# Identity-times-ones matmuls put ahead of five waits of TensorE in a hybrid decoder layer

## The chip, the cores and the metric

The kernel runs on one core of one Trainium2 chip. The metric is the device time of one execution in microseconds (us): 2514.37 us is the median of three runs of the kernel before, which took 2513.86, 2514.37 and 2521.84 us.

## The reference, cut to what matters

One decoder layer is applied to 576 tokens (a prompt of 512 and 8 sampled sequences of 8) with a model width of 2048, all in float32:

```
xn = rmsnorm(x, n1g);  z = xn @ w_in                  # 2048 x 6152
y_conv = rmsnorm(bg * conv3(cg * xt), conv_g)         # short gated convolution
h = mlstm(q, k, v, li, lf);  y_ml = sigmoid(o) * rmsnorm(h, ml_g)
x = x + concat(y_conv, y_ml) @ w_out
hn = rmsnorm(x, n2g)
x = x + (silu(hn @ wg) * (hn @ wu)) @ wd              # wg, wu: 2048 x 5632, wd: 5632 x 2048
y = rmsnorm(x, final_g)
```

The new convolution rows and the mLSTM states (C, n, m) are returned as well.

## The kernel before, in words

Tokens lie along the free dimension, as two halves of 288 columns. Every large product is made from three matmuls: each operand is split into a high and a low part (ScalarE copies the high part, VectorE subtracts to get the low part), and TensorE adds high x high, high x low and low x high into one PSUM bank.

The input projection and the output projection come first (lines 600 and 603). The change begins behind them, in the gate and up projections and in the first two thirds of the down projection. There a pair of token halves times a 2 x 2 block of weights is not made from eight half products but from seven, by sums and differences of blocks. One such set of seven is a *group*; its products are called p = 0 to 6 here. `product` (lines 828 to 842) issues one: 8 blocks of 128 rows, three matmuls each (lines 834, 836, 838), so 24 matmuls of 288 columns. p2, p4 and p6 go on in the bank that p0 began, p5 in the bank of p1.

There are 44 groups of gate and up (g = 0 to 43), and 16 groups of down (d = 0 to 15, g = 44 to 59, 8 to a column half of the hidden operand: PPC = 8). The token operands ophi and oplo (seven of each) stay the same for groups 0 to 43, change before d = 0, and change again before d = 8. At the start they are made while the last tile of the output projection ends. After the 16 groups, the rest of down (`down_block`, lines 929 to 947) multiplies the hidden operand as the stationary side with 512 columns of weights at a time.

What sets the order around the change is one instruction stream per engine, each in its own order, with semaphores:

- TensorE runs `first_group` (g = 0), then `group` for g = 1 to 43, then `down_group` for d = 0 to 15, then the loop over `down_block`. `group` waits ahead of p1 for `c12_ok`, ahead of p2 for `p1c_ok`, ahead of p6 for `c22_ok`, and so on; `product` itself waits for `g_lo`, the low part of its weights. A wait for `c22_ok` stands ahead of p6 of each group. It is raised by VectorE in `upper_up` (line 2124) or `add_block` (line 2237) as the first step of the *following* group's work on VectorE.
- VectorE makes the weights' sums (`weight_sum`, lines 2052 to 2065), their low parts (`product_low`, line 2070), the operands' low parts (`operand_low`, line 2080; `hidden_low`, line 2216), and reads the banks.
- ScalarE makes the high parts (line 1249 for weights, lines 1260 and 1316 for operands), copies a bank aside once p0, p1 and p2 are done (line 1267: p1c, p5c, u2c), and the sigmoid.
- SyncE issues the loads of weights and operands. Its loads of group 1 wait for `ss2_mm`, which TensorE raises after `norm_squares`, two float32 matmuls with a matrix of ones behind p2 of the first group.

`ident` and `ones` are 128 x 128 float32 tiles, written once at the start and not changed afterwards. `one(out, lhsT, rhs)` (line 608) is a single matmul.

Of the kernel before, what the change touches and what calls it, by code (L numbers as in the profile page):

```python
# [21 lines left out]
P = 128  # L22
# [38 lines left out]
def hybrid_trunk_step(nc, x_prompt, x_sample, state_conv, state_C, state_n, state_m, norm1_g, w_in,  # L61
# [38 lines left out]
    X_PIECES = ((0, 2), (2, 2), (4, 4), (8, 4), (12, 4))  # L100
    SMALLS = 10
    SQ_ACT = 4
    X_LAST = {k0 + n - 1: b for b, (k0, n) in enumerate(X_PIECES)}
    assert sum(n for _, n in X_PIECES) == KT
    QS = float(DK) ** -0.5
# [7 lines left out]
    NCH, PPC = FS // KT, KT // 2  # L113
# [5 lines left out]
    DOWN_BANK = (2, 3, 1, 4, 0, 5, 6, 7)  # L119

    with ExitStack() as ctx:
# [21 lines left out]
        ident = keep("ident", [P, P])  # L143
        ones = keep("ones", [P, P])
# [85 lines left out]
        u = take("u", TOK)  # L230
# [71 lines left out]
        ps = ctx.enter_context(nc.psum_tensor("ps", [P, 8, 512], F32))  # L302
# [277 lines left out]
        def _(pe):  # L580
# [241 lines left out]
            def norm_squares():  # L822
# [2 lines left out]
                    mm = one(ps[:, 6 + a, 0:HT], ones[:], ssq2[:, a, :])  # L825
                mm.then_inc(ss2_mm, 1)

            def product(m, u, p, bank, start, ks=(0, GK)):

                slot = (7 * u + p) % 3  # L830
                pe.wait_ge(g_lo, m * (7 * GU) + (7 * u + p + 1))
                out = ps[:, bank, 0:HT]
                for k in range(*ks):
                    pe.matmul(out, gw_ring[:, slot, 0, k, :], ophi[p][:, k, :], start=start and k == 0, stop=False,  # L834
                              skip_group_check=True)
                    pe.matmul(out, gw_ring[:, slot, 0, k, :], oplo[p][:, k, :], start=False, stop=False,  # L836
                              skip_group_check=True)
                    mm = pe.matmul(out, gw_ring[:, slot, 1, k, :], ophi[p][:, k, :], start=False, stop=k == GK - 1,  # L838
                                   skip_group_check=True)
                if ks[1] == GK:  # L840
                    mm.then_inc(g_used, 1)
# [12 lines left out]
            def group(m, u, first=False):  # L854
                g = m * GU + u
                bank_a, bank_b, bank_c = BANK_A[u % 3], 1, 4
                if first and u == 2:
                    pe.wait_ge(tile_read, I_FFN + 1)
                elif not first or u > 2:
                    pe.wait_ge(c21_ok, g - 2)  # L860
                product(m, u, 0, bank_a, True)
                pe.wait_ge(c12_ok, g)
                product(m, u, 1, bank_c, True)
                pe.wait_ge(p1c_ok, g + 1)
                product(m, u, 2, bank_a, False)
                pe.wait_ge(c11_ok, g)
                product(m, u, 3, bank_b, True)
                pe.wait_ge(u2c_ok, g + 1)
                product(m, u, 4, bank_a, False)
                pe.wait_ge(p5c_ok, g + 1)  # L870
                product(m, u, 5, bank_c, False)
                pe.wait_ge(c22_ok, g + 1)
                product(m, u, 6, bank_a, False)

            def first_group():

                bank_a, bank_b, bank_c = 2, 1, 4
                upto = ((0, GK - 1), (GK - 1, GK))
                for part, n in zip(upto, (GK - 1, GK)):
                    pe.wait_ge(b11_lo, n)  # L880
                    pe.wait_ge(tile_read, I_FFN)
                    product(0, 0, 0, bank_a, True, part)
                    pe.wait_ge(t1_lo, n)
                    pe.wait_ge(tile_read, I_FFN + 1)
                    product(0, 0, 1, bank_c, True, part)
                for p, bank, start, ready in ((2, bank_a, False, p1c_ok), (3, bank_b, True, None),
                                              (4, bank_a, False, u2c_ok), (5, bank_c, False, p5c_ok),
                                              (6, bank_a, False, c22_ok)):
                    if ready:
                        pe.wait_ge(ready, 1)  # L890
                    pe.wait_ge(op_lo, 3 * (p - 2) + 2)
                    product(0, 0, p, bank, start, (0, 4))
                    pe.wait_ge(op_lo, 3 * (p - 2) + 3)
                    product(0, 0, p, bank, start, (4, GK))
                    if p == 2:
                        norm_squares()

            def down_group(d):
                g = FT + d
                m, u = g // GU, g % GU  # L900
                bank_a, bank_b, bank_c = BANK_A[u % 3], 1, 4
                for p, bank, start, ready, n in ((0, bank_a, True, c21_ok, g - 2), (1, bank_c, True, c12_ok, g),
                                                 (2, bank_a, False, p1c_ok, g + 1), (3, bank_b, True, c11_ok, g),
                                                 (4, bank_a, False, u2c_ok, g + 1), (5, bank_c, False, p5c_ok, g + 1),
                                                 (6, bank_a, False, c22_ok, g + 1)):
                    pe.wait_ge(ready, n)
                    if d % PPC:
                        product(m, u, p, bank, start)
                    else:
                        before = 15 + 14 * (d // PPC) + 2 * p  # L910
                        pe.wait_ge(op_lo, before + 1)
                        product(m, u, p, bank, start, (0, 4))
                        pe.wait_ge(op_lo, before + 2)
                        product(m, u, p, bank, start, (4, GK))
                    if p == 3 and d > PPC:
                        turn_pair(d - 1)
# [13 lines left out]
            def down_block(x, n, j, t, start, stop):  # L930
# [16 lines left out]
                                       skip_group_check=True)  # L947
                return mm

            for n in range(2 * NBD * NCD):  # L950
                c, b, half = n // (2 * NBD), n % (2 * NBD) // 2, n % 2
                pe.wait_ge(dh_lo, 2 * c + half + 1)
                pe.wait_ge(d_lo, n + 1)
                for t in range(5):
                    x = 5 * (NBD * c + b) + t
                    if half == 0:
                        if x >= 8:
                            pe.wait_ge(d_read, x - 7)
                        elif x == 2:
                            pe.wait_ge(c11_ok, NG1)  # L960
                        elif x == 3:
                            pe.wait_ge(c12_ok, NG1)
                        elif x == 4:
                            pe.wait_ge(c21_ok, NG1)
                        elif x == 5:
                            pe.wait_ge(x1t_ok, KT)
                    mm = down_block(x, n, 2 * c + half, t, half == 0, half == 1)
                    if half == 1 and t < 4:
                        mm.then_inc(d_bank, 1)
                mm.then_inc(d_used, 1)  # L970
                if n == 0:
                    turn_pair(NCH * PPC - 1)
# [1492 lines left out]
```

## Time and profile before

| | us |
|---|---|
| median of three runs | 2514.37 |
| lowest and highest | 2513.86, 2521.84 |
| the profiled execution's own time | 2525.42 |
| its span, first to last instruction | 2523.5 |
| TensorE matmuls busy in the span | 2468.8 (98%) |
| VectorE busy | 1787.7 (71%) |
| ScalarE busy | 894.4 (35%) |
| mean granted TensorE clock | 0.99 of full speed |

The profile is of one execution. Times in its rows are microseconds from the start of the span, durations of single instructions nanoseconds where a row says so. Matmuls are pipelined, so the duration of a matmul row is longer than its distance from the next start; it is that distance that counts for the time. An arrow (<-) names what ended an engine's idle time, with the line that did it. [...]

### The profile page before, as it was taken

The numbers are of one execution on the slowest core, as the hardware profiler recorded it, in microseconds if no ns is written. First come the engines' busy times: TensorE is split into PE (matmuls) and PEld (weight loads), VectorE is DVE, ScalarE is ACT, GpSimd is POOL, SyncE is SP. The second block draws the span as 40 slices with busy tenths as digits, with TensorE's granted clock in tenths as the row PEclk, the third lists the DMA queues.
The fourth block names the chain that finished last, engine by engine and source line by source line (L and its number), as shares of the span: only waits on it lengthen the run. The fifth ranks groups of instructions, "written<-read, shape, count | busy, mean of one in ns | idle before, by whom it ended". The sixth has DMA issues, their size and how long they took to land.

```text
span 2523.5 us, 44736 instructions
## 1 busy us (share of the span) xinstructions
PE 2468.8 (98%) x17714; PEld 2410.7 (96%) x17714; DVE 1787.7 (71%) x2497; ACT 894.4 (35%) x1236; POOL 36.9 (1%) x59
## 2 busy tenths in 40 slices
PE   8999999999999998999999999999999899899998
PEld 7999999999999998999999999999999899899886
DVE  7576575575687668887777777877777966866435
ACT  5212222222233335344343433434444533544313
POOL 0000000000000000000000000000000000000100
PEclk9999999999999999999999999999999999999999
DMA  5333333333235665344343433434334645744722
GB/s 129 95 121 94 87 105 99 91 100 95 81 115 160 186 188 188 113 126 117 101 132 111 125 114 104 126 114 120 115 98 132 228 142 167 238 136 140 261 89 75
DMA packets 458924, 325.55 MB, mean 129 GB/s; under 512 B 14131, under 2 KB 429007, under 8 KB 456369
## 3 DMA queue, kind: packets, MB, share of 16 engines
q1 hardware_dynamic: 403704, 250.29, 33.7%
q10 hardware_dynamic: 51448, 58.42, 7.6%
q0 software_dynamic: 3584, 14.16, 1.5%
q8 instruction: 141, 2.31, 0.4%
q14 instruction: 47, 0.38, 0.0%
HBM read 264.49 MB, written 58.34 MB: 128 GB/s over the span
## 4 chain that ended last, share of the span: by engine, by line
PE 91%; DVE 5%; issue 1%; DMA 1%; ACT 1%; SPq 0%; DVEq 0%; ACTq 0%
PE ps L600 21%; PE ps L834 16%; PE ps L838 16%; PE ps L836 16%; PE ps L603 10%; PE ps L608 4%; PE ps L937 2%; PE ps L939 2%; PE ps L941 2%; DVE oplo L2216 1%; DVE gw_ring L2070 1%; DMA opraw<-hop 0%; PE ps L945 0%; DMA xtok<-in_x_sample_dram 0%; PE ps L946 0%
## 5 line engine op out<-in xcount | busy, mean ns | idle before, releaser
L834 PE MATMUL ps<-ophi,gw_ring 128*128 128x288 f32 x3360 | 999.8, 298 | 29.5 <-DVE cacc L2237 8.5
L836 PE MATMUL ps<-oplo,gw_ring 128*128 128x288 f32 x3360 | 995.0, 296 | 0.0
L838 PE MATMUL ps<-ophi,gw_ring 128*128 128x288 f32 x3360 | 993.2, 296 | 0.0
L834 PEld LDWEIGHTS ps<-ophi,gw_ring 128*128 128x128 f32 x3360 | 633.9, 189 | 33.9 <-DVE cacc L2237 9.2
L838 PEld LDWEIGHTS ps<-ophi,gw_ring 128*128 128x128 f32 x3360 | 636.6, 189 | 0.0
L836 PEld LDWEIGHTS ps<-oplo,gw_ring 128*128 128x128 f32 x3360 | 634.9, 189 | 0.1
L1002 ACT ACTIVATE whi<-wraw 128x512 fp32r<-128x512 f32 x256 | 160.7, 632 | 610.0 <-PE ps L603 466.2
L600 PE MATMUL ps<-xhi,whi 128*128 128x288 f32 x1536 | 334.0, 299 | 0.0
L600 PE MATMUL ps<-xlo,whi 128*128 128x288 f32 x1536 | 329.7, 296 | 0.0
L603 PE MATMUL ps<-xhi,wlo 128*128 128x288 f32 x1536 | 329.6, 296 | 0.0
L2070 DVE TENSOR_TENSOR gw_ring<-graw_a,gw_ring 128x1024 fp32r<-128x1024 f32 x200 | 244.7, 1224 | 119.2 <-ACT gw_ring L1249 118.7
L1249 ACT ACTIVATE gw_ring<-graw_a 128x1024 fp32r<-128x1024 f32 x200 | 211.6, 1058 | 279.8 <-PE ps L838 267.9
L1537 DVE TENSOR_TENSOR wlo<-wraw,whi 128x512 fp32r<-128x512 f32 x256 | 179.3, 701 | 140.5 <-ACT whi L1002 138.7
L600 PEld LDWEIGHTS ps<-xhi,whi 128*128 128x128 f32 x1536 | 248.3, 190 | 4.0 <-issue 3.0
L600 PEld LDWEIGHTS ps<-xlo,whi 128*128 128x128 f32 x1536 | 248.6, 190 | 0.0
L603 PEld LDWEIGHTS ps<-xhi,wlo 128*128 128x128 f32 x1536 | 248.5, 189 | 0.0
L2070 DVE TENSOR_TENSOR gw_ring<-wsum,gw_ring 128x1024 fp32r<-128x1024 f32 x120 | 146.6, 1221 | 87.8 <-ACT gw_ring L1249 87.8
L1532 DVE TENSOR_TENSOR wraw<-wraw,vecs 128x512 f32<-128x512 f32 x224 | 149.0, 683 | 43.4 <-DMA wraw<-in_w_in_dram 21.5
L1249 ACT ACTIVATE gw_ring<-wsum 128x1024 fp32r<-128x1024 f32 x120 | 126.8, 1056 | 123.8 <-PE ps L838 109.9
L2070 DVE TENSOR_TENSOR gw_ring<-graw_b,gw_ring 128x1024 fp32r<-128x1024 f32 x100 | 122.4, 1224 | 55.9 <-ACT gw_ring L1249 55.5
L1249 ACT ACTIVATE gw_ring<-graw_b 128x1024 fp32r<-128x1024 f32 x100 | 105.8, 1058 | 130.3 <-PE ps L838 128.2
L600 PE MATMUL ps<-mixhi,whi 128*128 128x288 f32 x512 | 109.9, 296 | 0.6 <-DVE wlo L1537 0.6
(329 smaller groups left out, 2566.7 us busy)
## 6 DMA issues: line engine op xcount, KB each, us to landing
wraw<-in_w_in_dram SPq DMA_DIRECT2D x96, 512.0 KB, 3.8
graw_a<-in_w_ffn_gate_dram SPq DMA_DIRECT2D x59, 512.0 KB, 3.7
graw_a<-in_w_ffn_up_dram SPq DMA_DIRECT2D x59, 512.0 KB, 4.9
graw_a<-in_w_ffn_down_dram SPq DMA_DIRECT2D x42, 512.0 KB, 5.7
wraw<-in_w_out_dram SPq DMA_DIRECT2D x32, 512.0 KB, 3.9
opraw<-hop SPq DMA_DIRECT2D x14, 1152.0 KB, 10.5
graw_b<-in_w_ffn_gate_dram SPq DMA_DIRECT2D x29, 512.0 KB, 3.7
graw_b<-in_w_ffn_up_dram SPq DMA_DIRECT2D x29, 512.0 KB, 4.5
```

The source lines that it names most:

```text
L600: pe.matmul(out[:, a, :], whi[:, q, s, :], moving[:, 2 * k + a, :], start=first and moving is hi, stop=False)
L603: mm = pe.matmul(out[:, a, :], wlo[:, q, s, :], hi[:, 2 * k + a, :], start=False, stop=last)
L608: one = lambda out, lhsT, rhs, start=True, stop=True: pe.matmul(out, lhsT, rhs, start=start, stop=stop)
L834: pe.matmul(out, gw_ring[:, slot, 0, k, :], ophi[p][:, k, :], start=start and k == 0, stop=False, skip_group_check=True)
L836: pe.matmul(out, gw_ring[:, slot, 0, k, :], oplo[p][:, k, :], start=False, stop=False, skip_group_check=True)
L838: mm = pe.matmul(out, gw_ring[:, slot, 1, k, :], ophi[p][:, k, :], start=False, stop=k == GK - 1, skip_group_check=True)
L937: pe.matmul(out, hhi[s][:, k, tok], dwhi[w][:, k, :], start=start and k == 0, stop=False, skip_group_check=True)
L1002: act.activation(whi[:, q, 0:n, :], wraw[:, q // 2, s0:s0 + n, :], ACT.Copy).then_inc(hi_done, 1)
L1249: act.activation(gw_ring[:, (7 * u + p) % 3, 0], source(u, p), ACT.Copy).then_inc(g_hi, 1)
L1532: tt(w, w, g, ALU.mult).then_inc(gained, 1)
L1537: tt(wlo[:, q, 0:n, :], wraw[:, q // 2, s0:s0 + n, :], whi[:, q, 0:n, :].bitcast(F32), ALU.subtract).then_inc(lo_done, 1)
L2070: tt(gw_ring[:, slot, 1], source(u, p), gw_ring[:, slot, 0].bitcast(F32), ALU.subtract).then_inc(g_lo, 1)
```

## The change

A helper `fill(n, bank)` issues n matmuls of `ident` (stationary) with `ones` (128 columns moving), each into the same 128 columns of one PSUM bank, each starting anew. Nobody reads what they write, and they neither wait for a semaphore nor raise one. They are issued in TensorE's stream at these places:

- 11 in `first_group`, behind p1 and ahead of the wait of p2;
- 10 in group 1 ahead of its p0, and 8 in group 1 behind p2, ahead of the wait of p3;
- 7 in d = 0 and in d = 8, behind p0 and ahead of the wait of p1;
- 10 in d = 1 and in d = 9, ahead of the wait of p0;
- 10 behind the last group of down, ahead of the first wait of the `down_block` loop.

These are 73 in all. All go to bank 5, but the last ten to bank 2 (`DOWN_BANK[0]`).

```diff
+    FILL_G0, FILL_G1, FILL_D, FILL_EXIT = 11, (10, 8), {(0, 1): 7, (1, 0): 10}, 10
...
+            def fill(n, bank=5):
+
+                for _ in range(n):
+                    one(ps[:, bank, 0:P], ident[:], ones[:])
+
...
+                if first and u == 1:
+                    fill(FILL_G1[0])
                 product(m, u, 0, bank_a, True)
                 pe.wait_ge(c12_ok, g)
                 product(m, u, 1, bank_c, True)
                 pe.wait_ge(p1c_ok, g + 1)
                 product(m, u, 2, bank_a, False)
+                if first and u == 1:
+                    fill(FILL_G1[1])
                 pe.wait_ge(c11_ok, g)
...
+                    if p == 2:
+                        fill(FILL_G0)
                     if ready:
                         pe.wait_ge(ready, 1)
...
+                    if (d % PPC, p) in FILL_D:
+                        fill(FILL_D[d % PPC, p])
                     pe.wait_ge(ready, n)
...
+            fill(FILL_EXIT, DOWN_BANK[0])
             for n in range(2 * NBD * NCD):
```

## Rows read from the trace of the kernel before

**Rows 1.** The page: busy time by engine; the chain that ended last, by engine.
```profile
PE 2468.8 (98%) x17714; PEld 2410.7 (96%) x17714; DVE 1787.7 (71%) x2497; ACT 894.4 (35%) x1236; POOL 36.9 (1%) x59
...
PE 91%; DVE 5%; issue 1%; DMA 1%; ACT 1%; SPq 0%; DVEq 0%; ACTq 0%
```

**Rows 2.** Busy time by stretch: PE, PEld, DVE, ACT, POOL, granted clock, DMA share, GB/s.
```profile
2000.00:2050.00 50.00, 50.00 (x378) 50.00 (x377) 35.21 (x41) 18.11 (x24) 0.00 (x0) 1.00 0.49 142
...
2200.00:2250.00 50.00, 50.00 (x383) 50.00 (x382) 34.27 (x43) 21.42 (x32) 0.00 (x0) 1.00 0.48 135
```

**Rows 3.** TensorE in order of time, groups 0 and 1: start, duration, idle before.
```profile
969.16 0.37 PE L834 MATMUL ps<-ophi,gw_ring 128*128 128x288 f32 x1 [3.65 <-ACT p1c L1267]
...
978.79 0.37 PE L834 MATMUL ps<-ophi,gw_ring 128*128 128x288 f32 x1 [0.53 <-DVE gw_ring L2070]
...
981.93 0.29 PE L838 MATMUL ps<-ophi,gw_ring 128*128 128x288 f32 x1
...
989.18 0.40 PE L834 MATMUL ps<-ophi,gw_ring 128*128 128x288 f32 x1 [3.22 <-DVE up L2124]
...
1003.15 0.40 PE L834 MATMUL ps<-ophi,gw_ring 128*128 128x288 f32 x1 [2.60 <-ACT p1c L1267]
...
1007.96 0.29 PE L834 MATMUL ps<-ophi,gw_ring 128*128 128x288 f32 x1
```

**Rows 4.** The chain that ended last, 973 to 1003 us: start, duration, what.
```profile
974.10 0.98 PE ps L608 x4
...
976.58 6.73 DMA graw_a<-in_w_ffn_up_dram
...
1002.71 0.40 ACT p1c L1267
```

**Rows 5.** VectorE in order of time, around its load wait in group 0.
```profile
973.68 1.22 DVE L2065 TENSOR_TENSOR wsum<-graw_a 128x1024 f32<-128x1024 f32 x1
...
983.43 1.23 DVE L2052 TENSOR_TENSOR wsum<-graw_b,graw_a 128x1024 f32<-128x1024 f32 x1 [1.04 <-DMA graw_a<-in_w_ffn_up_dram]
```

**Rows 6.** TensorE in order of time: float32 matmuls of 128 columns at full clock.
```profile
137.83 0.39 PE L608 MATMUL ps<-qa,cst 128*128 128x128 f32 x2
...
138.72 0.39 PE L608 MATMUL ps<-qa,cst 128*128 128x128 f32 x2
```

**Rows 7.** TensorE in order of time, from group 43 to d = 0.
```profile
1964.90 0.40 PE L834 MATMUL ps<-ophi,gw_ring 128*128 128x288 f32 x1 [2.43 <-DVE up L2124]
...
1979.91 0.37 PE L834 MATMUL ps<-ophi,gw_ring 128*128 128x288 f32 x1 [0.47 <-DVE gw_ring L2070]
...
1995.21 0.40 PE L834 MATMUL ps<-ophi,gw_ring 128*128 128x288 f32 x1 [3.13 <-DVE cacc L2237]
```

**Rows 8.** TensorE in order of time, from d = 8 to d = 9.
```profile
2167.90 0.38 PE L834 MATMUL ps<-ophi,gw_ring 128*128 128x288 f32 x1 [0.44 <-DVE gw_ring L2070]
...
2171.94 0.37 PE L834 MATMUL ps<-ophi,gw_ring 128*128 128x288 f32 x1 [0.61 <-DVE gw_ring L2070]
...
2182.17 0.61 PE L834 MATMUL ps<-ophi,gw_ring 128*128 128x288 f32 x1 [3.12 <-DVE cacc L2237]
...
2188.09 0.29 PE L834 MATMUL ps<-ophi,gw_ring 128*128 128x288 f32 x1
```

**Rows 9.** Busy time by stretch in d = 0 and d = 8 (columns as in Rows 2).
```profile
1996.00:1998.00 2.00, 2.00 (x18) 2.00 (x17) 2.00 (x4) 0.00 (x0) 0.00 (x0) 1.00 0.80 216
...
2184.00:2186.00 2.00, 2.00 (x10) 2.00 (x10) 2.00 (x4) 0.00 (x0) 0.00 (x0) 0.50 1.01 275
```

**Rows 10.** TensorE in order of time, the start of the `down_block` loop.
```profile
2355.58 0.80 PE L937 MATMUL ps<-dwhi,hhi 128*128 128x512 f32 x1 [3.09 <-DVE hs L2328]
...
2358.73 0.41 PE L939 MATMUL ps<-dwhi,hlo 128*128 128x512 f32 x1
2358.98 0.39 PE L941 MATMUL ps<-dwlo,hhi 128*128 128x512 f32 x1
```

**Rows 11.** TensorE alone by stretch, among float32 matmuls: PE, granted clock, DMA share, GB/s.
```profile
320.00:322.00 2.00, 2.00 (x9) 0.50 0.15 45
```

## The prediction

> **What bounds the kernel now.** I read the page first: matmuls fill 98% of the span and the chain that ended last is TensorE's for 91% [rows 1]. So a matmul added where TensorE does not wait lengthens the run by its own price, and one added inside a wait is free. The busy time by stretch shows which case holds: 50.00 of 50.00 us between the changes of operands [rows 2]. Then I read TensorE in order of time around each of the places, for three things: the wait, who ends it, and the distance between starts behind it. A product of 24 matmuls at full clock takes 3.27 us (978.79 to 981.93, plus 0.13 for the last) [rows 3]. [...]
>
> The waits that matter are 3.65 us ahead of p2 of group 0, 3.22 us ahead of its p6, 2.60 us ahead of p2 of group 1 [rows 3], 2.43 us ahead of p6 of group 43, 3.13 us ahead of p6 of d = 0 [rows 7], 3.12 us ahead of p6 of d = 8 [rows 8] and 3.09 us at the head of the `down_block` loop [rows 10]. Setting the diff beside this list decides the forecast: only the fills of group 0 and of the loop's head stand directly inside a long wait. Those of d = 1 and d = 9 stand behind the p6 that waited, not ahead of it.
>
> **The price of a fill.** It is not in the trace. The nearest rows are float32 matmuls of 128 columns with 128 stationary columns, each of which is a pair of instructions: four of them from 137.83 to 138.72 us, so 0.22 us each at full clock [rows 6]. Bounds: 0.11 us if it were one instruction of the pair, 0.45 us at half the clock. I take 0.22, which is the same operation. Then 7, 8, 10 and 11 fills cost 1.56, 1.78, 2.23 and 2.45 us.
>
> **Group 0, 11 fills.** They end 2.45 us into the wait of 3.65 us, and 1.2 us of waiting are left. I take it that the clock then stays, since waits of 0.53 us show no slow matmuls behind them [rows 3]; 1.2 us lies nearer to those than to 2.6. p2 had taken 4.94 us, from 969.16 [rows 3] to 974.10, where norm_squares follows [rows 4], and gets some 1.5 us shorter. Does that shorten the run? p3, p4 and p5 wait for VectorE and ScalarE, which are busy making operands there, so not directly. But the chain goes through it: norm_squares ends, SyncE issues the loads of group 1, the third of them runs for 6.73 us from 976.58 [rows 4], and VectorE had waited 1.04 us for it at 983.43. This load also needs a sum that VectorE ends at 974.9 [rows 5], which still lets it go 1.5 us earlier. So VectorE's wait disappears, and with it 1.04 us of its chain to p6. Term: -1.04, with 0 and -1.5 as ends.
>
> **Group 1.** The ten fills ahead of p0 are issued when p6 of group 0 is done, where nothing waits. They push p0 and p1 by 2.23 us into the wait of 2.60 us that follows. That wait is ended by ScalarE's copy p1c at 1002.71 [rows 4], behind the reciprocals and the square root; this chain needs p0 only for the copy itself, and p0 is still done over 3 us before it. So they cost nothing. They leave some 0.4 us of the wait, or 0.6 us when a shorter slow stretch comes before; without the cover they would cost 2.23. p2 should then run at full clock: it took 4.81 us (1003.15 to 1007.96) [rows 3] against 3.27. Term: -1.54. The eight fills behind p2 come where p3 had started without a wait. Its weights are ready, so they cost their full price: +1.78. In this group the change gives back what it wins.
>
> **d = 0 and d = 8, seven fills ahead of p1.** p1 and p2 are pushed by 1.56 us. Ahead of p3 waits of 0.47 us (d = 0) [rows 7] and 0.44 us (d = 8) take part of it, ahead of p4 of d = 8 another 0.61, and the last half a microsecond is gone before the wait of 3.12 us ahead of p6 [rows 8]. VectorE, which ends all of these, is busy without a break on operands' low parts and does not wait for p1 or p2. Term 0; with that cover gone, +3.1 for both. Nothing is won either: no long wait gets shorter except the one ahead of p6, and that one by nothing, since p5 still starts when VectorE is ready.
>
> **d = 1 and d = 9, ten fills ahead of p0.** p6 of the group before has just run, p0 followed it without a gap, and TensorE then works through without waiting (50.00 us of 50.00 in the stretches behind each) [rows 2]. The transition to d = 8 and that to the loop at the end start from TensorE's own progress (the hidden operands are reloaded when their products are done), so they move along. Term: 2 x 2.23 = +4.45, with 2.2 and 9 as ends by the price's bounds.
>
> **The loop's head, ten fills.** They fill 2.23 of 3.09 us. Before, the first seven matmuls took 3.15 us (2355.58 to 2358.73) against 7 x 0.25 = 1.75 us by the distance of the next two starts [rows 10]. Behind it TensorE sets the end. Term: -1.40, with 0 as the other end.
>
> **Sum:** -1.04 - 1.54 + 1.78 + 4.45 - 1.40 = +2.25 us. The profiled execution took 2525.42 us with 1.9 us around its span, so the changed kernel would take 2527.7 in such an execution. The median of the runs is 11 us lower than the profiled one; no term depends on that difference, so I add the sum to the median: **2516.6 us**. A measurement of this kernel can tell about 0.3%, or 7.5 us, from no change (the three runs lie 8.0 us apart), so this is a forecast of no change.
>
> **Rivals.**
> First, the clock falls elsewhere. The waits ahead of p6 of d = 0 and d = 8 are alike, 3.13 and 3.12 us, and neither gets a fill ahead of it. Behind the first the clock stayed 1.00, behind the second it was 0.50 [rows 9], and p6 took 5.92 us (2182.17 to 2188.09) [rows 8] instead of 3.27. That is 2.65 us on the path. Everything is shifted after the change: both may fall (2516.6 + 2.65 = 2519.3) or neither (2514.0). Chance 0.14 and 0.12.
> [...]
>
> Second, slower: the fills do not keep the clock up. Against them speaks that TensorE was busy without a gap with float32 matmuls from 320 to 322 us and yet had the clock at 0.50 [rows 11], so being busy alone is no proof; for them speaks that the matmuls of the price's rows ran one behind another at the distance of full clock [rows 6]. Then the three gains disappear and the unhidden fills remain: 2514.4 + 1.78 + 4.45 = 2520.6. If p6 of d = 0 also falls, 2523.3. It decides itself at p2 of group 0: distances of 0.24 us there in spite of the fills. Chance 0.15.
>
> Third, faster: the fills behind p2 of group 1 and in d = 1 and d = 9 are hidden, because VectorE's or SyncE's chain, not TensorE, sets the pace there. Then only the gains stay: 2514.4 - 3.98 = 2510.4. The full stretches of rows 2 speak against it. Chance 0.08.
>
> The forecast itself, within about 2 us, has 0.46; what is left, 0.05, goes to runs like the one of 2521.84.
>
> **How the numbers follow.** The range is 2510 to 2522: it takes in the third rival at its lower end, and at its upper end the first, and the second without a further fall. About 0.1 is left out above and less below. No case reaches 2506.8, where faster by over 0.3% begins: even with all gains, fills hidden and no fall at d = 8, it is 2507.7; I leave 0.05. Above 2521.9 lie the second rival with one more fall, fills at half clock, and a median drawn from the upper run: 0.12. Within 0.3%: 0.83.
>
> **What would show it.** Right: p2 of group 0 and of group 1 with starts 0.13 us apart; no wait of VectorE for the load of the up weights; p3 of group 1 starting some 1 us earlier than 1007.96; p0 of d = 1 and of d = 9 2.2 us behind p6; waits ahead of p6 of d = 0 and d = 8 still about 3 us. Wrong: clock at 0.50 behind the fills; a wait of TensorE in groups 1 to 5 or in d = 1 that takes the fills in; p6 of d = 0 starting later by the seven fills.

## The result, and the profile after

The changed kernel is slower: 2535.80 us in the median of 6 runs (2531.45 to 2541.15) against 2518.23 us for the kernel before on the same chip (2513.86 to 2525.31). The ratio is 1.0064, with a 95% interval of 1.0049 to 1.0080, so 12 to 20 us. The prediction was 2516.6 us, no change. The profiled execution took 2531.74 us, its span 2529.9 us.

The page after, busy time and the chain by engine, answers to [rows 1]:

```profile
PE 2473.3 (98%) x17860; PEld 2416.8 (96%) x17860; DVE 1787.1 (71%) x2497; ACT 894.9 (35%) x1236; POOL 36.4 (1%) x59
...
PE 90%; DVE 6%; issue 2%; ACT 1%; DMA 1%; SPq 0%; DVEq 0%; ACTq 0%
```

I cut both traces at TensorE events that exist in both. From p2 of group 0 to p3 of group 1 the time falls from 38.80 to 37.98 us. From p6 of group 43 to the end it grows from 558.6 to 561.9. Between the two, where the change has **not one line**, it grows from 956.9 to 974.3 us. (The work ahead of group 0 took 14 us less in this execution; its TensorE code is the same in both kernels, and the last section shows how much it scatters.)

Busy time of the middle of that stretch, before and then after (us, then PE, PEld, DVE, ACT, POOL, granted clock, DMA share, GB/s):

```profile
1200.00:1600.00 400.00, 395.96 (x2969) 395.27 (x2968) 313.62 (x372) 159.35 (x195) 0.00 (x0) 1.00 0.40 116
```
```profile
1200.00:1600.00 400.00, 387.06 (x2850) 385.56 (x2849) 301.10 (x356) 152.30 (x187) 0.00 (x0) 0.98 0.39 114
```

In the same 400 us TensorE is busy for 8.90 us less and has its clock at 0.98 instead of 1.00. It gets through 119 fewer matmuls, which at 0.133 us each (400.00 us for 3005 in e8 below) are 15.8 us. TensorE in order of time shows where. Before, there are exactly three waits over half a microsecond in this window:

```profile
1245.86 0.40 PE L834 MATMUL ps<-ophi,gw_ring 128*128 128x288 f32 x1 [1.14 <-DVE gw_ring L2070]
...
1381.97 0.40 PE L834 MATMUL ps<-ophi,gw_ring 128*128 128x288 f32 x1 [1.57 <-DVE gw_ring L2070]
...
1517.83 0.39 PE L834 MATMUL ps<-ophi,gw_ring 128*128 128x288 f32 x1 [1.32 <-DVE gw_ring L2070]
```

After, there are six, in three pairs:

```profile
1230.27 0.29 PE L844 MATMUL ps<-ophi,gw_ring 128*128 128x288 f32 x1
1233.39 0.51 PE L840 MATMUL ps<-ophi,gw_ring 128*128 128x288 f32 x1 [2.83 <-DVE gw_ring L2085]
1233.70 0.44 PE L842 MATMUL ps<-oplo,gw_ring 128*128 128x288 f32 x1
1233.94 0.44 PE L844 MATMUL ps<-ophi,gw_ring 128*128 128x288 f32 x1
1234.18 0.44 PE L840 MATMUL ps<-ophi,gw_ring 128*128 128x288 f32 x1
1234.42 0.44 PE L842 MATMUL ps<-oplo,gw_ring 128*128 128x288 f32 x1
1234.66 0.44 PE L844 MATMUL ps<-ophi,gw_ring 128*128 128x288 f32 x1
1234.90 0.44 PE L840 MATMUL ps<-ophi,gw_ring 128*128 128x288 f32 x1
1236.73 0.61 PE L842 MATMUL ps<-oplo,gw_ring 128*128 128x288 f32 x1 [1.39 <-issue]
...
1374.35 0.40 PE L840 MATMUL ps<-ophi,gw_ring 128*128 128x288 f32 x1 [2.40 <-issue]
...
1377.41 0.61 PE L842 MATMUL ps<-oplo,gw_ring 128*128 128x288 f32 x1 [1.86 <-issue]
...
1514.87 0.39 PE L840 MATMUL ps<-ophi,gw_ring 128*128 128x288 f32 x1 [2.57 <-DVE gw_ring L2085]
...
1517.93 0.61 PE L842 MATMUL ps<-oplo,gw_ring 128*128 128x288 f32 x1 [1.88 <-issue]
```

The three places lie 136 us apart before and 141 after, the time of six groups, and so they stand at the three jumps back of TensorE's loop over groups 6 to 29. Read the pair: a wait of 2.4 to 2.8 us at the jump, seven matmuls, a second wait "for issue" of 1.4 to 1.9 us, and behind that starts 0.24 us apart, the clock at 0.50 (at the first jump between the two as well). The six sum to 12.93 us, before's three to 4.03; the difference is the 8.90 us of the windows. The low clock makes the rest: it stands at 0.50 for 17.1 us behind the three pairs, half of which, 8.5 us, is loss. That the same kind of wait is once put down to VectorE's gw_ring and once to "issue" is a warning about the first name.

**Theory.** TensorE stands at the jump because its next instructions have not come. The page counts 44736 instructions before and 45028 after, so a fill is four instructions; 29 of the 73 fills stand ahead of the loop and push it 116 instructions further into TensorE's code. Instructions come in packets of 16.4 KB (queue q8: 141 packets, 2.31 MB before). TensorE has 36273 records in that trace, 257 to a packet, so my estimate is that a packet is one block of about 256 instructions. The loop's body has 2069 instructions in the compiled program, 8 x 256 + 21 (the trace has 2068 of them from one jump to the next), so where its head lies in a block fixes two things: how many instructions are left behind the target of the jump, and how far behind a block's border the jump itself stands. **Rivals:** the fills' own multiplications; a clock that falls because of them; waits for VectorE, as the trace names them.

So far this is a supposition: the page shows neither why TensorE stands at a jump nor what the loop's place does to it. The runs below test both.

### The profile page after: what moved, and what is told of

It reads as the page before. It is cut to its first block, busy times and chain, and to the rows that moved or that the text cites. A ratio compares the mean times of both kernels' runs of the same rounds, so it can differ in the third digit from the quotient of the medians.

```text
span 2529.9 us, 45028 instructions
## 1 busy us (share of the span) xinstructions
PE 2473.3 (98%) x17860; PEld 2416.8 (96%) x17860; DVE 1787.1 (71%) x2497; ACT 894.9 (35%) x1236; POOL 36.4 (1%) x59
## 3 DMA queue, kind: packets, MB, share of 16 engines
q8 instruction: 146, 2.39, 0.4%
## 4 chain that ended last, share of the span: by engine, by line
PE 90%; DVE 6%; issue 2%; ACT 1%; DMA 1%; SPq 0%; DVEq 0%; ACTq 0%
PE ps L601 21%; PE ps L840 17%; PE ps L844 16%; PE ps L842 16%; PE ps L604 10%; PE ps L609 3%; PE ps L951 2%; PE ps L955 2%; PE ps L953 2%; DVE gw_ring L2085 1%; DVE oplo L2231 1%; DVE oplo L2095 0%; DMA opraw<-hop 0%; DMA xtok<-in_x_sample_dram 0%; PE ps L959 0%
## 5 line engine op out<-in xcount | busy, mean ns | idle before, releaser
L844 PE MATMUL ps<-ophi,gw_ring 128*128 128x288 f32 x3360 | 995.3, 296 | 0.0
```

## The experiments

All times are medians, with the ratio to the kernel before, measured beside it, and its 95% interval. The three stages are differences of starts in the one profiled execution of each kernel, in us: A from p2 of group 0 to p3 of group 1, B from there to p6 of group 43, C from there to the end of the span.

| kernel | A | B | C | median | ratio |
|---|---|---|---|---|---|
| before | 38.80 | 956.94 | 558.59 | 2518.23 | 1 |
| changed | 37.98 | 974.26 | 561.88 | 2535.80 | 1.0064 (1.0049 to 1.0080) |
| changed again (e12) | 39.49 | 969.43 | 561.44 | 2538.65 | 1.0065 (1.0052 to 1.0079) |
| e1 waits for fills | 38.28 | 972.01 | 560.68 | 2535.04 | 1.0061 (1.0043 to 1.0080) |
| e2 head at 128 | 37.97 | 958.74 | 562.02 | 2524.54 | 1.0020 (1.0007 to 1.0032) |
| e3 fills behind only | 36.91 | 957.51 | 562.42 | 2522.63 | 1.0010 (0.9998 to 1.0022) |
| e4 hint | 37.97 | 957.04 | 561.63 | 2524.10 | 1.0019 (1.0008 to 1.0030) |
| e5 head at 0 | 37.98 | 964.50 | 560.46 | 2528.19 | 1.0051 (1.0030 to 1.0072) |
| e6 head at 228 | 37.99 | 960.83 | 561.48 | 2527.13 | 1.0033 (1.0018 to 1.0047) |
| e7 border ahead of jump | 37.98 | 964.47 | 560.74 | 2526.01 | 1.0036 (1.0024 to 1.0048) |
| e8 hint, head at 128 | 37.98 | 953.13 | 561.90 | 2518.24 | 0.9999 (0.9985 to 1.0012) |
| e9 before, hint, head at 128 | 38.32 | 952.42 | 558.93 | 2514.06 | 0.9967 (0.9956 to 0.9978) |
| e10 two fills, hint, head at 128 | 36.28 | 953.33 | 557.49 | 2514.54 | 0.9967 (0.9956 to 0.9977) |
| e11 three fills, both loops | 36.27 | 953.32 | 557.51 | 2506.09 | 0.9939 (0.9926 to 0.9953) |

**e1: the place without the fills.**

```diff
-    FILL_G0, FILL_G1, FILL_D, FILL_EXIT = 11, (10, 8), {(0, 1): 7, (1, 0): 10}, 10
+    FILL_G0, FILL_G1, FILL_D, FILL_EXIT = 11, (10, 8), {}, 0
...
-                for _ in range(n):
-                    one(ps[:, bank, 0:P], ident[:], ones[:])
+                for _ in range(8 * n):
+                    pe.wait_ge(tile_read, 1)
```

> Each of the 29 fills ahead of the loop over groups 6 to 29 is replaced by eight waits that are already met, which the compiler packs into four instructions, so TensorE's loop lies at the same place in its code as in the changed kernel (116 instructions further than before), but no fill multiplies anything; the 27 fills behind the loop are left out. Theory (the loop's place in the code costs the time at its three jumps back): the stretch from p3 of group 1 to p6 of group 43 takes 972 to 976 us, as in the changed kernel (974.3) and not as before (956.9), and the whole is 14 to 20 us slower than before. Rival (the fills' multiplications, or a clock that falls elsewhere because of them): no fill is left, so the stretch takes 956 to 958 us and the whole is within 4 us of before.

(The fills left out behind the loop are 44, not 27: those of d = 0 and d = 1 come again at d = 8 and d = 9.) The page counts 44852 instructions, 116 more than before, for 29 x 8 = 232 added waits, so eight of them are four instructions, the number of one fill; matmuls are 17714, as before. Stage B takes 972.0 us and the whole 1.0061 of before, with no fill in the program. The first jump, TensorE in order of time:

```profile
1239.71 0.40 PE L840 MATMUL ps<-ophi,gw_ring 128*128 128x288 f32 x1 [2.64 <-DVE gw_ring L2085]
...
1243.05 0.61 PE L842 MATMUL ps<-oplo,gw_ring 128*128 128x288 f32 x1 [2.15 <-issue]
```

The same pair, and again at the other two jumps (1.46 + 1.45 and 2.50 + 1.87 us). The fills' multiplications do not make the loss; 116 instructions of another kind make it as well.

**e2: the fills without the place.**

```diff
-            with pe.Fori(1, FS // GU) as m:
+            with nc.Fori(1, FS // GU, engines=bass.OrderedEngineSet([pe.engine]), head_slot={pe.engine: 128}) as m:
```

> The changed kernel with every fill, and the head of TensorE's loop over groups 6 to 29 put at slot 128 of a block of 256 instructions, near where the packets of instructions suggest that it was before. Theory (place of the loop): the stretch from p3 of group 1 to p6 of group 43 falls from 974.3 to 956 to 959 us and the whole comes out 15 to 19 us faster than the changed kernel, 0 to 5 us slower than before, near the 2.25 us that the prediction's sum gives. Rival (the fills): all fills are still there, so the stretch stays at 972 to 976 us and the whole 14 to 20 us slower than before.

Stage B falls to 958.7 us with one wait at each jump:

```profile
1240.32 0.39 PE L840 MATMUL ps<-ophi,gw_ring 128*128 128x288 f32 x1 [1.52 <-DVE gw_ring L2085]
...
1376.46 0.40 PE L840 MATMUL ps<-ophi,gw_ring 128*128 128x288 f32 x1 [1.61 <-issue]
...
1512.31 0.40 PE L840 MATMUL ps<-ophi,gw_ring 128*128 128x288 f32 x1 [1.32 <-DVE gw_ring L2085]
```

That is before's state again, and the fills' rival is dead on both sides. The whole is 1.0020 of before, about 5 us (2 to 8); the prediction's 2.25 us lies at the lower end. Against the changed kernel's 1.0064 that is some 11 us, less than the 15 to 19 expected: the whole shows the stage's 15.5 us only roughly.

**e3: only the fills behind the loop.**

```diff
-    FILL_G0, FILL_G1, FILL_D, FILL_EXIT = 11, (10, 8), {(0, 1): 7, (1, 0): 10}, 10
+    FILL_G0, FILL_G1, FILL_D, FILL_EXIT = 0, (0, 0), {(0, 1): 7, (1, 0): 10}, 10
```

> Only the fills behind the loop (d=0, d=1, d=8, d=9 and the ten ahead of down's blocks); the loop lies where it lay before. Theory (place of the loop): the stretch from p3 of group 1 to p6 of group 43 takes 956 to 958 us; the part behind it is 3.0 to 3.5 us longer than before (561.9 against 558.6), as in the changed kernel, and so the whole is 2 to 4 us slower than before. Rival (the fills behind the loop carry the loss by what they do to the clock): the whole is 10 us or more slower than before.

Stage B 957.5, stage C 562.4 (+3.8; 3.0 to 3.5 were expected), the whole 1.0010, about 2.5 us: the fills behind the loop do not carry the loss.

**e4: the jump announced.**

```diff
-            with pe.Fori(1, FS // GU) as m:
+            with nc.Fori(1, FS // GU, engines=bass.OrderedEngineSet([pe.engine]), hint_back_edge=True) as m:
```

> [...] Theory (TensorE stands at each jump back for instructions that have not come): the waits of 2.4 to 2.8 us and the second ones of 1.4 to 1.9 us behind the three jumps go or shrink below 0.5 us, the clock stays at 1.00, the stretch from p3 of group 1 to p6 of group 43 takes 952 to 957 us, and the whole is 17 to 22 us faster than the changed kernel. If only the first of the two waits goes, the stretch takes 960 to 968 us. Rival (VectorE's copies, named by the profile as what released the first of these waits, or the fills): nothing changes, 972 to 976 us.

The page counts 45032 instructions for the changed kernel's 45028, one more in each of the four rounds, and the trace has a record for it on TensorE's sequencer (PEldq), with its least, median and longest duration in ns:

```profile
L935 PEldq BRANCH_PREFETCH_HINT  x4: 40/40/45, 1106.1 to 1513.4; - x4
```

What it sets off in the chip the trace does not show, only what changes with it: from the first jump back to the second q8 brings nine packets of instructions (1239.22 to 1374.53 us) where the changed kernel has eleven (1228.12 to 1369.50), and the three jumps last 2.85, 3.27 and 3.10 us. The waits shrink to 0.77, 1.20 and 1.03 us and the second ones go; stage B 957.0. So stage B lands at the upper end of the expectation, but no wait is below 0.5 us, and the whole is only some 11 us faster than the changed kernel. An instruction of 40 ns that does no work of the kernel and touches no semaphore takes three quarters of the waiting away (12.93 us to 3.00); a wait for VectorE's data would not care. Why the second waits go although as few instructions lie behind the target as before stays open.

**e5 to e7: what about the place costs.** The diff is that of e2 with another slot; e7 has in the loop's body also:

```diff
                 for w in range(GU):
                     group(m, w)
+                    for _ in range(16):
+                        pe.wait_ge(tile_read, 1)
```

> The changed kernel with every fill, the loop's head at slot 0 of a block of 256 instructions: all 256 lie behind the target in its block, and the jump back lies 20 instructions behind a block's border. Theory (a stall at the jump for the target's block, longer when a border has just been crossed; a second one when few instructions are left behind the target): one stall at each of the three jumps, 1.3 to 2.8 us, no second one, clock at 1.00 right behind it; p3 of group 1 to p6 of group 43 takes 957 to 963 us. Rival (any place other than that of before costs some 17 us): 972 to 976 us.

> As before this, with the head at slot 228: 28 instructions are left in the target's block, and the jump back lies at slot 248, in front of a border and not behind one. Theory A (the few instructions behind the target make the loss): each jump has a second wait of 0.7 to 1.5 us some 12 matmuls behind the first, and the stretch takes 962 to 972 us. Theory B (the border ahead of the jump makes it): one stall of 1.1 to 1.6 us at each jump, no second one, 956 to 959 us. Both theories true: the first stall is as short as in B and the second is there.

> As before this, with the head at slot 190 (66 instructions left behind the target) and 96 waits that are already met, 48 instructions, spread over the six groups of the loop's body, so that the jump back lies at slot 2, right behind a border. Theory A (few instructions behind the target): one stall of 1.1 to 1.6 us at each jump. Theory B (the border): one stall of 2.4 to 2.9 us at each jump and no second one. The added instructions themselves may cost 0 to 10 us over the four rounds, so the stalls decide, not the whole.

The first jump of e5, the first of e6, and the second of e7:

```profile
1240.61 0.60 PE L840 MATMUL ps<-ophi,gw_ring 128*128 128x288 f32 x1 [2.55 <-DVE gw_ring L2085]
```
```profile
1241.89 0.40 PE L840 MATMUL ps<-ophi,gw_ring 128*128 128x288 f32 x1 [1.21 <-DVE gw_ring L2085]
...
1244.71 0.40 PE L842 MATMUL ps<-oplo,gw_ring 128*128 128x288 f32 x1 [0.83 <-issue]
```
```profile
1376.77 0.39 PE L840 MATMUL ps<-ophi,gw_ring 128*128 128x288 f32 x1 [2.57 <-DVE gw_ring L2087]
```

Each theory accounts for a wait of its own, but e7 does not bear out the one of the border. With the jump in front of a border (e6) the first wait is 1.21, 1.20 and 1.36 us; with the jump 20 instructions behind one (e5) it is 2.55, 2.65 and 2.39. In e7 (2 behind) it is 2.04, 2.57 and 2.50, which looks alike and is not. The trace has a record for the jump itself, COMPARE_BRANCH, on TensorE's sequencer (PEldq). For the three jumps back its durations in ns (least, median, most), in the order before, changed, e5, e6, e7:

```profile
L921 PEldq COMPARE_BRANCH  x3: 3317/3507/3755, 1242.3 to 1514.1; - x3
```
```profile
L935 PEldq COMPARE_BRANCH  x3: 4582/4751/5013, 1228.1 to 1509.9; - x3
```
```profile
L935 PEldq COMPARE_BRANCH  x3: 4575/4728/4832, 1235.6 to 1512.8; - x3
```
```profile
L935 PEldq COMPARE_BRANCH  x3: 3320/3355/3542, 1238.2 to 1511.8; - x3
```
```profile
L935 PEldq COMPARE_BRANCH  x3: 3340/3802/3875, 1234.5 to 1509.7; - x3
```

When such a jump begins, 17 matmuls, 2.28 us of work, are still ahead of TensorE, in every kernel that waits there but e7; what the jump takes beyond that is the wait, give or take 0.2 us. The jumps of e7 take hardly longer than those of before. But eight of its added instructions stand right ahead of the jump, 0.1 us apart, and leave only 1.40 us of work there. So its longer waits are the doing of the added instructions, and a border 2 instructions ahead of the jump did not lengthen it.

The second wait comes with few instructions behind the target alone: in e6 0.83, 0.83 and 0.77 us, in e5 and e7 none. In e6 it comes after 13 matmuls, which with their loads are 26 instructions of the 28 that are left in the block. In the changed kernel it comes after seven, so, with the same two others, its head lay at about slot 240 and its jump just behind a border: it got both. Before, 116 instructions earlier, it got neither.

The instruction queue shows what the longer jumps have in common. Packets, MB and share of 16 engines in one microsecond: the changed kernel from 1229 to 1230, then e6 from 1239 to 1240, both about 1 us ahead of the jump's last matmul:

```profile
q8 instruction: 2, 0.03, 22.7%
```
```profile
q8 instruction: 1, 0.02, 6.0%
```

In the changed kernel two packets run side by side, 22.7% of 16 us = 3.6 us of engine time for both, against 1.0 us for one alone. All 56 jumps back of over 1 us in the 14 traces (the loop over the heads included) divide by it: in 47 one packet starts within 2 us of the jump, and they take 2.85 to 3.88 us; in nine there are two, and they take 4.58 to 5.01. The nine are all three of the changed kernel and of e5, two of e1 and one of e12. So with one and the same code the second packet comes or stays away; the place makes it likely, not certain. The trace does not name a packet's content, so what the second one holds is not shown.

Stage B of e5 and e7 (964.5, about 11 us above that of e8 below) holds more than their waits (7.6 and 7.1 us): behind two of the three jumps the clock is at 0.50, for 6.8 us in sum in each, half of it loss; e7's has its added instructions besides. e5's expectation missed on that (clock at 1.00, at most 963), and e6's by 1.2 us on the other side (960.8, from 962): there the clock stayed up.

**e8: announced, and in a good place.**

```diff
-            with pe.Fori(1, FS // GU) as m:
+            with nc.Fori(1, FS // GU, engines=bass.OrderedEngineSet([pe.engine]), head_slot={pe.engine: 128}, hint_back_edge=True) as m:
```

> The changed kernel with every fill, the loop's head at slot 128 and the instruction that names the jump ahead of time. Theory (TensorE waits at the jumps for instructions alone): the stall at each jump falls from the 1.3 to 1.6 us of the head at 128 without it to below 0.6 us, p3 of group 1 to p6 of group 43 takes 953 to 956 us, and the whole is 2 to 5 us faster than with the head at 128 alone, within 3 us of before. Rival (the wait is for VectorE's gw_ring, as the profile names it): the stall stays at 1.1 us and more.

Busy time of the same 400 us as above:

```profile
1200.00:1600.00 400.00, 400.00 (x3005) 400.00 (x3004) 317.38 (x376) 160.47 (x197) 0.00 (x0) 1.00 0.41 119
```

No wait is left at any jump, and the jump itself takes a tenth of what it took (3.32 to 3.75 us before, 3.50 to 3.80 in e2):

```profile
L935 PEldq COMPARE_BRANCH  x3: 349/354/373, 1241.4 to 1510.0; - x3
```

The instruction queue changes with it: from the first jump back to the second, q8 brings ten packets in before (1242.28 to 1377.95 us) and in e2 (1236.35 to 1372.40), nine here (1241.44 to 1375.68) and in e9 (1233.26 to 1367.50).

So even before's 4.03 us were waits for instructions (e9 below, without any fill, has none either, its jumps last 0.35 to 0.37 us), and the name gw_ring in their rows was wrong: VectorE's copies are ready all the same. Stage B 953.1, the whole level with before.

**e9 to e12: the fills alone, and a better kernel.** e9 is the kernel before with e8's loop. e10 is e8 with the fills cut to

```diff
+    FILL_G0, FILL_G1, FILL_D, FILL_EXIT = 11, (0, 0), {}, 10
```

and e11 has `11, (10, 0), {}, 10`, and for the loop over the heads

```diff
-            with pe.Fori(0, H - 1) as h:
+            with nc.Fori(0, H - 1, engines=bass.OrderedEngineSet([pe.engine]), head_slot={pe.engine: 128}, hint_back_edge=True) as h:
```

> The kernel before, without any fill, with the loop's head at slot 128 and the instruction that names the jump ahead of time. Theory (its own three stalls of 1.1 to 1.6 us at the jumps are the fetch of the target's block): they go, p3 of group 1 to p6 of group 43 takes 953 to 954 us instead of 956.9, and the whole is 3 to 5 us faster than before. Against this kernel the changed one with the same loop (the run with the head at 128 and the hint) then tells what the fills alone cost: by the prediction's sum 2.25 us, by the stages of the changed kernel's profile (group 0 to p3 of group 1, 0.2 us less; p6 of group 43 to the end, 3.3 us more) 3.1 us. Rival (before's stalls are waits for VectorE's gw_ring): stage and whole stay as before, within 2 us.

> The fills that the prediction's sum prices as a gain and that stand in one wait each: the eleven ahead of p2 of group 0 and the ten ahead of down's blocks; the others left out; the loop with its head at 128 and the hint. By the sum: 1.04 + 1.40 = 2.4 us faster than the kernel before with the same loop, so 5.5 to 7.5 us faster than before in all. If the gain of the warmer stretches is given back at the next wait, as in groups 0 and 1 of the changed kernel, it is within 1.5 us of the kernel before with the same loop.

> As the run with the two fills of gain, with the ten ahead of p0 of group 1 added (not the eight behind its p2, nor any ahead of d=0 to d=9), and the loop over the heads also with its head at 128 and the hint. Its two jumps back stand 1.1 us each before: these go, 2 us. The ten fills ahead of p0 of group 1 stand wholly inside a wait and the clock is up for p0 to p2: group 0's start to p3 of group 1 takes 47.5 to 48.5 us instead of 50.0. The whole is 7 to 10 us faster than before. If the entry of the first loop costs a fetch of its own, 1 to 2 us of this are missing.

> The changed kernel once more, unedited, beside the other runs of this call. Theory (place of the loop): two stalls at each jump again, 4 us and more in sum in most of them, p3 of group 1 to p6 of group 43 at 970 to 976 us, the whole 13 to 20 us slower than before and 14 to 21 us slower than the kernel before with the hint. Were the 17 us of the first profile an accident of that execution, the stage would be below 962 us here.

e12 repeats the loss: 1.0065, stage B 969.4 (970 to 976 were expected), a pair of waits at each jump (2.54 + 2.15, 1.16 + 2.03, 1.36 + 1.63 us). e9 gains 8.2 us (6 to 11), more than the 3 to 5 expected; its stage B gains 4.5, and where the rest comes from is open. Against it the fills with the same loop (e8) cost, by the stages, -0.34 + 0.71 + 2.97 = 3.3 us; by the whole 0.32% or 8 us, give or take 4. e10 is as fast as e9 as a whole, while its stages sum to 2.6 us less (-2.04 + 0.91 - 1.44): expected 2.4, but the whole does not show it. A part of stage A's difference is not the fills' doing, as the next section shows.

e11 is the fastest: 2506.09 us, 0.9939 of before (0.9926 to 0.9953), so 12 to 19 us better than before and more than the 7 to 10 expected. Its A to C equal those of e10, so the ten fills ahead of p0 of group 1 bring nothing. What is new is the loop over the heads. TensorE there, around its two jumps (columns as above), first e10, then e11:

```profile
230.00:260.00 30.00, 28.55 (x212) 27.77 (x211) 14.19 (x26) 7.66 (x14) 1.20 (x3) 1.00 0.27 72
410.00:440.00 30.00, 28.48 (x212) 27.78 (x210) 14.16 (x26) 7.66 (x14) 1.15 (x3) 1.00 0.27 72
```
```profile
230.00:260.00 30.00, 30.00 (x224) 29.47 (x224) 14.92 (x26) 7.67 (x14) 1.89 (x3) 1.00 0.31 81
410.00:440.00 30.00, 30.00 (x225) 29.47 (x224) 15.45 (x31) 7.67 (x14) 1.89 (x3) 1.00 0.27 72
```

Its waits, 1.45 and 1.52 us in e10, are gone. That is 3.0 of the 8.5 us between the two medians. The other 5.5 are not shown by one execution each, but the clock is the likely place: in e11's profile the granted clock is 1.00 over both rounds of that loop (348.96 us), in e10's it is 0.97 (362.03 us), and the 12 others need 353.5 to 361.4. The mean granted clock of all runs, 0.9946 in e11's five and 0.9928 in e10's eight, makes it some 4.6 us, an estimate (the missing share of 2510 us), though e10's runs scatter from 0.989 to 0.995. Whether the announced jump keeps the clock up there is not shown.

## Why the prediction was wrong

**The step that failed** is the list of waits that decides the forecast ("The waits that matter are ..."), and the sum made from it, which has terms only at places where the diff has a line. The three waits of 1.14, 1.57 and 1.32 us at the start of groups 12, 18 and 24 were in the trace of before, with VectorE's gw_ring as releaser. The list passes over them, and the sum puts them at nothing, as no edit touches them. They were TensorE's jumps back, and every instruction added ahead of the loop moves them. The missing term is +17.3 us in this profile, +12.5 in e12 and +15.1 in e1 (stage B less 956.94); the prediction's own sum was +2.25. None of the rivals held it: the nearest, a clock that falls elsewhere, named two waits that are not these.

**The terms that were priced held.** In group 0, TensorE in order of time after the change, answering to [rows 3]:

```profile
951.92 2.62 PE L609 MATMUL ps<-ones,ident 128*128 128x128 f32 x22
955.74 0.37 PE L840 MATMUL ps<-ophi,gw_ring 128*128 128x288 f32 x1 [1.20 <-ACT p1c L1282]
...
965.38 0.38 PE L840 MATMUL ps<-ophi,gw_ring 128*128 128x288 f32 x1 [1.45 <-DVE gw_ring L2085]
...
974.76 0.40 PE L840 MATMUL ps<-ophi,gw_ring 128*128 128x288 f32 x1 [2.22 <-DVE up L2139]
...
978.06 2.39 PE L609 MATMUL ps<-ones,ident 128*128 128x128 f32 x20
980.21 0.38 PE L840 MATMUL ps<-ophi,gw_ring 128*128 128x288 f32 x1
...
988.73 0.40 PE L840 MATMUL ps<-ophi,gw_ring 128*128 128x288 f32 x1 [1.90 <-ACT p1c L1282]
...
992.02 1.95 PE L609 MATMUL ps<-ones,ident 128*128 128x128 f32 x16
993.72 0.38 PE L840 MATMUL ps<-ophi,gw_ring 128*128 128x288 f32 x1
```

Ten fills take 2.15 us (978.06 to 980.21), 0.215 each; predicted 0.22. The wait left ahead of p2 is 1.20 us; predicted 1.2. Behind it starts stand 0.13 us apart, and not 0.24 as behind the jumps' waits, where the clock is at 0.50; so the second rival, fills that don't keep the clock, is wrong. VectorE no longer waits for the load of the up weights, and p2 to p6 of group 0 shrinks from 20.02 to 19.02 us: -1.00, predicted -1.04. From p6 to p2 of group 1 it stays 13.97 us, so the ten fills are hidden. From p2 to p3 it goes from 4.81 to 4.99, +0.18 against -1.54 + 1.78 = +0.24. The seven fills of d = 0 cost nothing, as predicted: from p6 of group 43 to p6 of d = 0 it is 30.31 us in both kernels.

Right sizes don't make the gains real in every execution, though. Stage A was 38.80, 38.32 and 36.91 us in three executions without fills there (before, e9, e3), since the clock behind the same waits sometimes falls and sometimes does not: it stood at 0.50 for three stretches of 3.4 us in before, for two in e9 (from 961.2 and 995.3 us) and for 6.8 us from 961.0 in e3. With all fills it was 37.97 to 37.99 in seven of eight. The forecast of -0.80 came from one execution, in which the clock had fallen behind all three waits (969.5, 990.0 and 1003.7 us); the mean of the three is 38.0, and so on the mean all fills together gain nothing here.

From d = 0 to the end, answering to [rows 7, 8, 10]:

```profile
1967.98 0.61 PE L840 MATMUL ps<-ophi,gw_ring 128*128 128x288 f32 x1 [3.77 <-DVE up L2139]
...
1998.29 0.61 PE L840 MATMUL ps<-ophi,gw_ring 128*128 128x288 f32 x1 [3.13 <-DVE cacc L2252]
...
2003.01 2.40 PE L609 MATMUL ps<-ones,ident 128*128 128x128 f32 x20
2005.16 0.38 PE L840 MATMUL ps<-ophi,gw_ring 128*128 128x288 f32 x1
...
2188.91 0.40 PE L840 MATMUL ps<-ophi,gw_ring 128*128 128x288 f32 x1 [2.04 <-DVE cacc L2252]
...
2193.72 2.39 PE L609 MATMUL ps<-ones,ident 128*128 128x128 f32 x20
2195.87 0.38 PE L840 MATMUL ps<-ophi,gw_ring 128*128 128x288 f32 x1
...
2360.21 2.39 PE L609 MATMUL ps<-ones,ident 128*128 128x128 f32 x20
2363.45 0.50 PE L951 MATMUL ps<-dwhi,hhi 128*128 128x512 f32 x1 [0.85 <-DVE hs L2343]
```

The fills of d = 1 and d = 9 cost their full 2.15 us each, so the third rival is wrong too. Over all profiles, stage C is 561.6 us with them (mean of nine) and 557.5 without (e10, e11): +4.1, predicted +4.45. The ten ahead of down's blocks, with 0.85 us of their wait left, bring it from 558.6 and 558.9 (before, e9) to 557.5: -1.3, predicted -1.40. (e1, without fills there too, took 560.7: its clock was at 0.50 for 24.7 us of the stage, against 18.0 and 19.6, so single executions leave about 2 us open here.) The first rival, whose two chances of 0.14 and 0.12 were my estimate, came in part: the clock behind p6 of d = 0 fell (p6 to the fills 4.72 us instead of 3.27), and behind d = 8, where 2.04 us of the wait were left, it fell for a shorter time (4.81 instead of 5.92), +1.45 and -1.11, nearly nothing. Stage C as a whole: +3.3, predicted +3.05. That stages A and C together come to -0.82 + 3.29 = +2.47 us for the predicted +2.25 is luck in part, since falls of the clock that no term had cancel in it.

So with the loop put back where it loses nothing extra, the change costs about 5 us (2 to 8; e2), 3.3 by the stages of e8 and e9, with the prediction's 2.25 at the lower end; in stage B 12 to 17 us more come from where its instructions lie.

## What to carry to other kernels

Here the two long loops of TensorE (2069 and over 2600 instructions) waited at every jump back that was not announced, 1.0 to 2.8 us, and the short one (under 400) at none. How much it was depended on the loop's place in the code: each instruction added ahead of a loop moves that place (116 here, and 12 to 17 us with them), so an edit before a long loop can have a term inside the loop. Look in the trace for waits that come once per round, whoever they are put down to; if the named engine had long been done, suspect instructions, read how long the jump's own record lasts, and test it by announcing the jump and fixing the head's slot. An instruction added right ahead of the jump shortens the work that covers it (1.40 us for 2.28 in e7), so such an edit tests two things at once. Fill an engine's wait only where the fill stands ahead of the wait itself, and judge its gain over several executions, since the clock behind one and the same wait falls in one and not in the next (stage A without fills: 36.91 to 38.80 us).

## What the runs showed of the hardware that I had not expected

- A jump back of TensorE in the loop over groups 6 to 29 made it wait 1.1 to 1.6 us (before, e2, e3, e6 and three jumps of e1 and e12), and 2.4 to 2.8 us in nine of the 12 jumps with a block's border some 4 to 20 instructions ahead of them (changed, e12, e1, e5). There was a second wait of 0.8 us with 28 instructions left behind the target (e6), of 1.4 to 2.2 us with about 16 (changed, e12, e1). Announced and with the head at slot 128 the jump costs nothing that shows (e8: 400.00 of 400.00 us busy).
- The jump itself lasts 2.85 to 3.88 us with one packet of instructions on its way and 4.58 to 5.01 with two, 0.34 to 0.39 announced and with the head at slot 128 (e8 to e11), and 0.21 to 0.24 in the loop over the output projection, whose rounds of 396 records show no wait at any jump.
- Behind the longer waits the clock is at 0.50 for a while, 17.1 us in sum in the changed kernel's loop, which cost about as much again as the added waiting (8.5 and 8.90 us).
- The same TensorE code ahead of group 0 took 943.9 to 958.0 us in 13 profiled executions of kernels that don't touch it. The two rounds of the loop over the heads make up to 8.5 us of that (353.5 to 362.0 us, with the clock at 0.50 for 3.4 to 20.5 us of them). A difference of a few us between two single profiles, taken over the whole, says nothing; taken stage by stage it says more, though stage C without fills still scattered by 2 us (558.6 to 560.7 in before, e9 and e1).
